# The merge of the two branches moved into the recurrent stage's block, its last head in column pieces, and semaphore counts that start at zero

## The chip, the cores and the metric

One core of one Trainium2 chip. The time is the device time of one launch in microseconds, all outputs written; lower is better. All times of the trace are microseconds from the start of the profiled execution.

## What is computed

A one-layer encoder step for a prompt of 1024 tokens and a sample of 64, 1088 tokens (T) in all, width 1024:

```python
h = rms_norm(x, norm_mix) * (1 + sc1) + sh1
hq, hf, hi, hog, gq, gk, gv, gog, glr, ga, gb = jnp.split(h @ w_in, split_at, axis=-1)
o_hg, s_hg = chunked_gated_linear_attention(q_hg, k_hg, hi, log_f, state_hgrn)     # 4 heads
o_gla, s_gla = chunked_gated_linear_attention(q_gla, gk, gv, log_g, state_gla)     # 4 heads
o = o * rsqrt(mean(o * o) + eps) * onorm * silu(gate)                              # both branches, per head
merged = sigmoid(ga) * (o_hg @ w_br_a) + sigmoid(gb) * (o_gla @ w_br_b)
x = x + g1 * (merged @ w_out)
x = x + g2 * hierarchical_moe(rms_norm(x, norm_ffn) * (1 + sc2) + sh2)             # 32 experts, 2 per token
y = rms_norm(x, norm_final)
```

Every product with a weight matrix is done as three matmuls of rounded parts (high x high, high x low, low x high; `split_matmul`, L131 to L135). So each operand is first split: a copy into a reduced type gives the high half, a subtraction the low half.

## The kernel before

Each stage is a block: the five engines run their own list of instructions and meet at the block's end, where all semaphores of the stage are cleared (`Stage.clear`, L121). The stages in order: conditioning (`condition`, names c_), the recurrent stage (`mixers`, x_), the merge (`merge`, m_), output projection and router (`out_router`, o_), experts (e_), overflow (v_), and the last norm (`combine`, z_). In each block SP first adds START = 20 to every semaphore of the stage, one instruction each (`raise_to_start`, L126), and every wait is written as `after(n)` or `landed(n)`, which add START.

**The recurrent stage** keeps the conditioned input h on chip as two halves, `h_hi` and `h_lo`, [128, 8, T] each. It goes through six units u: two of the GLA branch with two heads each, four of the HGRN branch with one head each. For a unit PE projects columns of `w_in` (`project`), each name in three column pieces (364, 364, 360) of 24 matmuls; GpSimd (POOL) makes the high half of each weight block (L510), VectorE (DVE) the low half (`next_low`, L1031); ScalarE (ACT) copies each piece out of PSUM (L652). Then the unit runs over nine tiles of tokens, j = 0 to 8 for an HGRN unit. Per j: PE turns tile j + 1 (L536, L538) and computes its scores (L552, L555), does a projection piece where the table `filled` puts one, then the outputs and the state product of tile j (L576 to L578). DVE masks the scores of tile j + 1 (L999, L1004, L1006: two reductions) and advances the state by tile j (L1019), which the outputs of j + 1 wait for. ACT copies tiles and outputs out of PSUM. Of the last unit (u = 5) the second gate block, x1, is projected in these gaps, its three pieces at j = 0, 3 and 6.

After the last tile: ACT squares the head's output, PE forms the mean over the 128 channels in three pieces (L585), ACT takes logarithm (L768) and exponential (L772), DVE multiplies by it and by the gate (L989, L992), and the row goes to scratch memory, like the seven head rows before (`scratch_mix`) and the 16 gate rows (`scratch_gate`). ACT waits for all of these to land, and the block ends.

**The merge** loads the eight head rows [128, T] back over ACT's queue through three buffers, splits them (L1180 on ACT, L1195 on DVE), and loops over the eight column blocks of 128, two per round of a hardware loop. Per column block and piece PE computes branch a (12 matmuls), then branch b (12), into two banks each, DVE multiplies each by its gate and adds (L1203, L1205, L1207); after the third piece ACT makes the high half (L1187) and DVE the low half (L1209) of the merged row. Weights of the block are halved by POOL alone (L1169, L1172). The first product of a column block waits for the last gate of the block before:

```python
pe.wait_ge(w_lo_done, after(2 * i + j + 1))
for c, (c0, n) in enumerate(COLS):

    pe.wait_ge(b_gated, after(n0 + max(c - 1, 0)))
```

## Time and profile before

| | |
|---|---|
| median of 3 runs | 1918.81 us (1918.67 to 1918.93) |
| the profiled execution | 1918.63 us, of which the span is 1916.8 |
| PE busy | 1617.3 us (84%), 10704 matmuls |
| DVE busy | 1274.5 us (66%) |
| ACT busy | 953.3 us (50%) |
| POOL busy | 323.6 us (17%) |
| granted TensorE clock, mean | 0.924 of 2.4 GHz |
| read from memory, written | 316.71 MB, 44.38 MB |

A line of a timeline is: start, duration, engine, line of the kernel, operation, what it writes <- what it reads, partitions x elements, count, and in brackets how long the engine had been idle and what ended that. SPq and ACTq are issues of transfers on these engines' queues. A line of the split into windows gives the busy time of each engine with its number of instructions, then the granted clock (1.00 is 2.4 GHz, 0.50 is 1.2 GHz), the busy share of the DMA engines and GB/s.

### The profile page before, as it was taken

Reading aid. Unit: us, or ns where it says so; the run is one execution under the profiler, and the core shown is the slowest. Engines: PE = TensorE matmul, PEld = TensorE weight load, DVE = VectorE, ACT = ScalarE, POOL = GpSimd, SP = SyncE. Lnnn points to the kernel's source line nnn. Section 1 sums busy time; section 2 is a strip of 40 time slices with the busy share of each in tenths; the row PEclk is TensorE's granted clock in tenths of the full one; section 3 lists DMA queues with packets and bytes.
Section 4 is the critical chain, followed back from the end, with each engine's and each line's share of the span. In section 5 each row is a group of like instructions: output and inputs, shape, how many; then the busy total and the mean of one; then the engine's idle time right before and its main releaser. Section 6 shows DMA issues by size and latency. Waiting matters only on the chain. (4 is left out here: it accounts for less than half of the span.)

```text
span 1916.8 us, 26572 instructions
## 1 busy us (share of the span) xinstructions
PE 1617.3 (84%) x10704; PEld 1413.7 (74%) x10704; DVE 1274.5 (66%) x1507; ACT 953.3 (50%) x1159; POOL 323.6 (17%) x186
## 2 busy tenths in 40 slices
PE   4579999999899998985696996499999999999800
PEld 2459989988789898984696785388888888887600
DVE  2534368267658575855454436789999999998727
ACT  2724234332625353443102211478888888888623
POOL 0100001000101010100220000134442332322113
PEclk8789999999999999998698998699999999999955
DMA  8722101201111202111542534699999999999546
GB/s 337 292 57 68 35 12 64 88 25 35 60 47 36 70 23 73 34 51 52 182 137 90 201 121 136 234 344 370 377 376 382 378 360 372 367 371 373 200 177 234
DMA packets 189073, 347.06 MB, mean 181 GB/s; under 512 B 18290, under 2 KB 74202, under 8 KB 187868
## 3 DMA queue, kind: packets, MB, share of 16 engines
q1 hardware_dynamic: 171676, 308.48, 45.4%
q10 hardware_dynamic: 7392, 19.06, 2.6%
q0 software_dynamic: 9888, 17.88, 2.5%
q8 instruction: 83, 1.36, 0.3%
q14 instruction: 34, 0.28, 0.0%
HBM read 316.71 MB, written 44.38 MB: 188 GB/s over the span
## 5 line engine op out<-in xcount | busy, mean ns | idle before, releaser
L133 PE MATMUL x_psum_proj<-h_hi,x_w_hi 128*128 128x364 f32 (+1 forms) x1056 | 362.7, 343 | 23.6 <-ACT x_v L652 11.8
L134 PE MATMUL x_psum_proj<-h_lo,x_w_hi 128*128 128x364 f32 (+1 forms) x1056 | 351.3, 333 | 0.0
L135 PE MATMUL x_psum_proj<-h_hi,x_w_lo 128*128 128x364 f32 (+1 forms) x1056 | 351.0, 332 | 0.0
L133 PEld LDWEIGHTS x_psum_proj<-h_hi,x_w_hi 128*128 128x128 f32 x1056 | 202.1, 191 | 32.5 <-ACT x_v L652 12.7
L134 PEld LDWEIGHTS x_psum_proj<-h_lo,x_w_hi 128*128 128x128 f32 x1056 | 202.4, 192 | 2.3
L135 PEld LDWEIGHTS x_psum_proj<-h_hi,x_w_lo 128*128 128x128 f32 x1056 | 202.1, 191 | 0.0
L510 POOL CAST x_w_hi<-x_w 128x1024 fp32r<-128x1024 f32 x44 | 73.1, 1661 | 664.6 <-PE x_psum_proj L135 662.2
L1751 POOL DMA_INDIRECT scratch_y<-e_y,all_tbl x32 | 79.6, 2486 | 392.3 <-ACT e_y L1825 367.8
L1006 DVE TENSOR_REDUCE x_sc<-x_diag 64x64 f32<-64x448 f32 x136 | 126.9, 933 | 1.1
L133 PE MATMUL e_psum_g<-e_g_hi,e_x_hi 128*128 128x512 f32 x256 | 105.9, 414 | 19.3 <-DVE e_x_lo L1901 18.9
L999 DVE TENSOR_TENSOR x_diag<-x_psum_sc,all_shapes 128x448 f32<-128x448 f32 (+1 forms) x72 | 44.6, 620 | 97.8 <-PE x_psum_sc L555 93.9
L1031 DVE TENSOR_TENSOR x_w_lo<-x_w,x_w_hi 128x1024 fp32r<-128x1024 f32 x44 | 53.6, 1221 | 83.6 <-POOL x_w_hi L510 83.5
L133 PE MATMUL e_psum_y<-e_d_hi,e_hid_hi 128*128 128x512 f32 x256 | 103.3, 404 | 5.4 <-DVE e_d_lo L1896 5.4
L134 PE MATMUL e_psum_g<-e_g_lo,e_x_hi 128*128 128x512 f32 x256 | 102.3, 400 | 0.0
L135 PE MATMUL e_psum_g<-e_g_hi,e_x_lo 128*128 128x512 f32 x256 | 101.8, 398 | 0.0
L134 PE MATMUL e_psum_y<-e_d_lo,e_hid_hi 128*128 128x512 f32 x256 | 100.6, 393 | 0.0
L135 PE MATMUL e_psum_y<-e_d_hi,e_hid_lo 128*128 128x512 f32 x256 | 100.6, 393 | 0.0
L135 PE MATMUL e_psum_u<-e_u_hi,e_x_lo 128*128 128x512 f32 x256 | 99.8, 390 | 0.0
L133 PE MATMUL e_psum_u<-e_u_hi,e_x_hi 128*128 128x512 f32 x256 | 99.6, 389 | 0.0
L134 PE MATMUL e_psum_u<-e_u_lo,e_x_hi 128*128 128x512 f32 x256 | 99.6, 389 | 0.0
L1745 POOL DMA_INDIRECT e_xg<-scratch_h,all_src x32 | 65.6, 2051 | 197.1 <-DVE e_xg L1854 165.4
L652 ACT ACTIVATE x_x<-x_psum_proj 128x364 f32<-128x364 f32 (+1 forms) x48 | 22.1, 469 | 136.4 <-PE x_psum_proj L135 136.3
(322 smaller groups left out, 3887.2 us busy)
## 6 DMA issues: line engine op xcount, KB each, us to landing
mg_ring_hi<-in_w_e_gate SPq DMA_DIRECT2D x34, 1024.0 KB, 14.3
mg_ring_lo<-in_w_e_down SPq DMA_DIRECT2D x34, 1024.0 KB, 15.1
mg_ring_hi<-in_w_e_up SPq DMA_DIRECT2D x32, 1024.0 KB, 11.9
mg_ring_lo<-in_w_e_up SPq DMA_DIRECT2D x32, 1024.0 KB, 13.6
mg_ring_lo<-in_w_e_gate SPq DMA_DIRECT2D x30, 1024.0 KB, 14.3
mg_ring_hi<-in_w_e_down SPq DMA_DIRECT2D x30, 1024.0 KB, 14.3
c_w<-in_w_ada SPq DMA_DIRECT2D x12, 2048.0 KB, 15.3
x_w<-in_w_in SPq DMA_DIRECT2D x44, 512.0 KB, 3.9
```

Of the source, the lines that this page charges most:

```text
L133: nc.tensor.matmul(out, lhs[0], rhs[0], start=start, stop=False)
L134: nc.tensor.matmul(out, lhs[0], rhs[1], start=False, stop=False)
L135: return nc.tensor.matmul(out, lhs[1], rhs[0], start=False, stop=stop)
L510: nc.gpsimd.tensor_copy(w_hi[:, n % 2], w[:, n % 2]).then_inc(w_hi_done, 1)
L652: nc.scalar.activation(dst[:, c0:c0 + n], p_proj[:, e % 2, 0:n], ACT.Copy).then_inc(proj_kept, 1)
L999: V.tensor_tensor(diag[0:n, j % 2], p_sc[0:n, j % 2, 0:NL * 64].rearrange("p (l t) -> p l t", t=64), masks[0:n], ALU.mult).then_inc(sc_mas ...
L1006: red = V.tensor_reduce(sc[h0:h0 + 64, j % 2, h0:h0 + 64], diag[h0:h0 + 64, j % 2].rearrange("p l t -> p t l"), AX.X, ALU.add)
L1031: V.tensor_tensor(w_lo[:, n % 2], w[:, n % 2], w_hi[:, n % 2].bitcast(F32), ALU.subtract).then_inc(w_lo_done, 1)
L1745: nc.gpsimd.indirect_dma_start(out=xg[:, e % 2, :], out_offset=None, in_=h2_d, in_offset=bass.IndirectOffsetOnAxis(ap=src[:, e:e + 1], axi ...
L1751: nc.gpsimd.indirect_dma_start(out=y_d, out_offset=bass.IndirectOffsetOnAxis(ap=tbl[:, e:e + 1], axis=0), in_=y[:, e % 2, :], in_offset=No ...
```

## The change

The merge becomes the tail of the recurrent stage's block; the stage between is gone, and its hardware loop is written out. In its parts:

- **Places.** The merged halves `mg_hi`, `mg_lo` get a fixed place at the top of the memory, over buffers that the last unit no longer needs (k, q, b, ke, qe, v1, g1, the levels); the sum `mg_sum` lies where `mg_lo` will be written. The head rows come back into the place of `h_lo` (`land`), once the last projection is done, and their halves take the place of `h_hi` and `h_lo`. Weights go through the stage's own two buffers: high half on POOL, low half on DVE. Gate rows go into buffers of the unit.
- **Seven rows instead of eight.** Rows 4 to 7 (branch b) and 0 to 2 come from scratch; row 3, the head of the last unit, stays on chip and is normed, gated and split in three column pieces.
- **Order on PE.** x1 of the last unit is projected at j = 0, 1, 2. Branch b of column block 0 starts before the outputs of the last tile; the mean squares stand between its pieces; then branch a without row 3, then with it. Blocks 1 to 7: three pieces of b, then three of a, in three banks each.
- **DVE.** Four of the low halves of head rows stand in the last unit at j = 4 to 7, three behind it; the low weight half of block 0 stands at j = 1, that of block i + 1 behind the first a gate of block i.
- **ACT.** The logarithms of the last gate row move to j = 6 to 8; the last merged row is split by pieces.
- **Counts from zero.** `raise_to_start` is called only in the overflow stage (whose loops wait on registers); everywhere else waits are for n itself, and `reach` leaves out a wait for 0.

The core of the diff (waits that only lose START are shown once; the functions `last_square`, `mix_low`, `last_output`, `last_low`, `gate_b`, `gate_a`, `merged_low` hold one or two instructions with their waits, as described above):

```diff
+def reach(eng, sem, n):
+        eng.wait_ge(sem, n)
 ...
-            raise_to_start(sp, s)
 ...
-                    sp.wait_ge(w_lo_done, after(n - 1))
+                    reach(sp, w_lo_done, n - 1)
 ...
 
 
+        if u + 1 == NU:
+            return [g for some in groups[j:j + 1] for g in some]
 ...
+        land = h.over("land", "lo", 0, [P, KD, T])
+        gates = [(v[1], g[1])] + [(t1, tg) if i % 2 else (x[0], x[1]) for i in range(1, KD)]
 ...
+        NB, LAST, MIX_ROWS = KD // 2, HG_HEADS - 1, [4, 5, 6, 7, 0, 1, 2]
+        bank_a, bank_b = [p_sc[:, 0], p_sc[:, 1], p_o[:, 1]], [p_proj[:, 0], p_proj[:, 1], p_o[:, 0]]
 ...
+            def branch_weights(i):
+                n = len(loads) + i
+                sp.wait_ge(w_lo_done, n - 1)
+                for half in range(2):
+                    sp.dma_start(w[:, n % 2, half * NB:(half + 1) * NB], w_branch[half][:, :, i * P:(i + 1) * P]).then_inc(w_in[n % 2], 16)
+            def gate_rows(i):
+                for half in range(2):
+                    sp.dma_start(gates[i][half][:, :], gate_d[i + half * KD]).then_inc(gate_in[i % 2], 16)
+            branch_weights(0)
+            branch_weights(1)
+            sp.wait_ge(gate_out[0], 16 * (G0[NU] // 2))
+            sp.wait_ge(gate_out[1], 16 * (G0[NU] // 2 - 1))
+            sp.wait_ge(o_out[1], out_landed(NU, 1))
+            gate_rows(0)
+            sp.wait_ge(proj_done, len(order))
+            sp.wait_ge(o_out[0], out_landed(NU - 1, 0))
+            for n, row in enumerate(MIX_ROWS):
+                sp.dma_start(land[:, row, :], mix_d[row]).then_inc(land_in[n // NB], 16)
+            branch_weights(2)
+            sp.wait_ge(last_scaled, NC)
+            sp.wait_ge(x_dve, G0[NU])
+            gate_rows(1)
+            sp.wait_ge(gate_out[1], 16 * (G0[NU] // 2))
+            gate_rows(2)
+            for i in range(3, KD):
+                branch_weights(i)
+                sp.wait_ge(piece_done, (i - 1) * NC)
+                gate_rows(i)
 ...
+            def branch_high(i):
+                n = len(loads) + i
+                pool.wait_ge(w_in[n % 2], 16 * (len(loads) // 2 + 2 * (i // 2 + 1)))
+                if i < 2:
+                    pool.wait_ge(proj_done, place[loads[n - 2], NC - 1] + 1)
+                else:
+                    pool.wait_ge(a_done, (i - 1) * NC)
+                nc.gpsimd.tensor_copy(w_hi[:, n % 2], w[:, n % 2]).then_inc(w_hi_done, 1)
+            branch_high(0)
+            branch_high(1)
+            for n, row in enumerate(MIX_ROWS):
+                pool.wait_ge(land_in[n // NB], 16 * NB if n < NB else 16 * (len(MIX_ROWS) - NB))
+                nc.gpsimd.tensor_copy(h_hi[:, row, :], land[:, row, :]).then_inc(mix_hi_done, 1)
+            for i in range(2, KD):
+                branch_high(i)
 ...
+            def branch_b(i, c):
+                pe.wait_ge(w_lo_done, len(loads) + i + 1)
+                if i:
+                    pe.wait_ge(b_gated, (i - 1) * NC + c + 1)
+                elif c < 2:
+                    pe.wait_ge(proj_kept, len(order))
+                else:
+                    pe.wait_ge(o_kept, J0[NU])
+                for row in range(NB, KD):
+                    if i == 0 and c == 0:
+                        pe.wait_ge(mix_lo_done, row - NB + 1)
+                    m = branch_product(i, row, c, bank_b[c], row == NB, row == KD - 1)
+                m.then_inc(b_done_m, 1)
+            def branch_a(i, c, rows):
+                if i:
+                    pe.wait_ge(a_gated, (i - 1) * NC + c + 1)
+                elif c < 2:
+                    pe.wait_ge(sc_masked, J0[NU])
+                    pe.wait_ge(cross_ready, X0[NU])
+                for row in rows:
+                    if i == 0 and c == 0 and row != LAST:
+                        pe.wait_ge(mix_lo_done, NB + row + 1)
+                    if i == 0 and row == LAST:
+                        pe.wait_ge(last_lo, c + 1)
+                    m = branch_product(i, row, c, bank_a[c], row == 0, row == LAST)
+                if row == LAST:
 ...
                     for (of, name), c in filled(u, j):
                         project(of, name, c)
+                    if u + 1 == NU and j + 1 == NS[u]:
+                        branch_b(0, 0)
                     outputs(u, j)
+            branch_b(0, 1)
+            last_square(0)
+            last_square(1)
+            branch_b(0, 2)
+            last_square(2)
-            for c in range(NC):
-                mean_square(NU - 1, 0, c)
+            for c in range(NC):
+                branch_a(0, c, range(LAST))
+            for c in range(NC):
+                branch_a(0, c, [LAST])
+            for i in range(1, KD):
+                for c in range(NC):
+                    branch_b(i, c)
+                for c in range(NC):
+                    branch_a(i, c, range(NB))
 ...
+                nc.scalar.activation(t1[:, c0:c0 + n], t1[:, c0:c0 + n], ACT.Exp, scale=-0.5).then_inc(last_exp, 1)
+            for c, (c0, n) in enumerate(COLS):
+                act.wait_ge(last_ready, c + 1)
 ...
+                    if u + 1 == NU and NB <= j < 2 * NB:
+                        mix_low(j - NB)
                 if u + 1 < NU:
                     decay_sum(u + 1)
+            for n in range(NB, len(MIX_ROWS)):
+                mix_low(n)
+            last_output(0)
+            last_output(1)
+            last_low(0)
+            last_output(2)
+            last_low(1)
+            last_low(2)
+            gate_x(NU - 1, NX[NU - 1] - 1)
+            for i in range(KD):
+                dve.wait_ge(gate_in[i % 2], 32 * (i // 2 + 1))
+                for c in range(NC):
+                    gate_b(i, c)
+                if i:
+                    merged_low(i - 1, 0, T)
+                for c in range(NC):
+                    gate_a(i, c)
+                    if c == 0:
+                        next_low()
+                    if i + 1 == KD and c:
+                        merged_low(i, *COLS[c - 1])
+            merged_low(KD - 1, *COLS[NC - 1])
-            gate_x(NU - 1, NX[NU - 1] - 1)
-            output(NU - 1, 0)
 ...
-def merge(nc, a, mix_d, gate_d, m_hi, m_lo):
 ...
-            m_hi, m_lo = m.sb("hi", [P, KD, T], F32R), m.sb("lo", [P, KD, T], F32R)
-            merge(nc, a, scratch["mix"], scratch["gate"], m_hi, m_lo)
```

How the engines' lists change. VectorE at the end of the last unit, before (L1019 is the state update, L974 the gate row, L989 and L992 the head's output; then the merge's block with the head rows' low halves):

```order
L1019 SCALAR_TENSOR_TENSOR x_state<-x_state,x_eb_last,x_psum_u 128x128 x2
L974 SCALAR_TENSOR_TENSOR x_x<-x_x,x_tg 128x1088
L989 TENSOR_TENSOR x_v<-x_v,x_t 128x1088
L992 SCALAR_TENSOR_TENSOR x_v<-x_v,all_onorm,x_g 128x1088
L91 UNCONDITIONAL_BRANCH
L1190 UNCONDITIONAL_BRANCH
L1195 TENSOR_TENSOR m_mix_lo<-m_mix,m_mix_hi 128x1088 x8
L1196 UNCONDITIONAL_BRANCH
L1196 ISA
```

and after the change, at the same place behind the head rows' low halves (L1190 and L1193 are an output piece, L1199 its low half, L1117 the gate row, L1206 a gate of branch b, L1212 of branch a, L1174 the low half of weights):

```order
L1193 SCALAR_TENSOR_TENSOR x_v<-x_v,all_onorm,x_g 128x364
L1199 TENSOR_TENSOR h_lo<-x_v,h_hi 128x364
L1190 TENSOR_TENSOR x_v<-x_v,x_t 128x360
L1193 SCALAR_TENSOR_TENSOR x_v<-x_v,all_onorm,x_g 128x360
L1199 TENSOR_TENSOR h_lo<-x_v,h_hi 128x364
L1199 TENSOR_TENSOR h_lo<-x_v,h_hi 128x360
L1117 SCALAR_TENSOR_TENSOR x_x<-x_x,x_tg 128x1088
L1206 TENSOR_TENSOR mg_sum<-x_g,x_psum_proj 128x364 x2
L1206 TENSOR_TENSOR mg_sum<-x_g,x_psum_o 128x360
L1212 TENSOR_TENSOR x_v<-x_v,x_psum_sc 128x364
L1214 TENSOR_TENSOR mg_sum<-mg_sum,x_v 128x364
L1174 TENSOR_TENSOR x_w_lo<-x_w,x_w_hi 128x1024
```

The head rows' low halves and the head's output now stand in one list without a block's end between them, and the weights of block 1 come behind all of them. SP's queue, before (the block's end and the loop's head lie between the weights of the projections, L496, and those of the merge):

```order
L496 DMA x_w<-in_w_in 128x8x128 x44
L91 UNCONDITIONAL_BRANCH
L1145 UNCONDITIONAL_BRANCH
L1148 UNCONDITIONAL_BRANCH
L1148 ISA
L1154 ISA
L1154 DMA m_w<-in_w_br_a 128x4x128
L1155 DMA m_w<-in_w_br_b 128x4x128
```

and after (L524 are branch weights, L528 gate rows, L539 head rows):

```order
L517 DMA x_w<-in_w_in 128x8x128 x44
L524 DMA x_w<-in_w_br_a 128x4x128
L524 DMA x_w<-in_w_br_b 128x4x128
L524 DMA x_w<-in_w_br_a 128x4x128
L524 DMA x_w<-in_w_br_b 128x4x128
L528 DMA x_v<-scratch_gate 128x1088
L528 DMA x_g<-scratch_gate 128x1088
L539 DMA h_land<-scratch_mix 128x1088 x7
L524 DMA x_w<-in_w_br_a 128x4x128
L524 DMA x_w<-in_w_br_b 128x4x128
L528 DMA x_t<-scratch_gate 128x1088
L528 DMA x_tg<-scratch_gate 128x1088
```

The gate rows of block 0 and two blocks of weights now stand ahead of the head rows, the gate rows of blocks 1 and 2 behind them.

## Rows read from the trace of the kernel before

**Rows 1.** Split into windows around the seam and in the merge, columns as told above.

```profile
910.00:920.00 10.00, 0.15 (x1) 0.18 (x2) 3.88 (x3) 3.31 (x4) 3.88 (x2) 0.50 1.01 353
...
920.00:930.00 10.00, 5.51 (x17) 4.88 (x18) 4.44 (x4) 3.97 (x4) 3.96 (x2) 0.50 1.04 358
...
960.00:980.00 20.00, 19.38 (x117) 19.08 (x116) 11.61 (x16) 1.66 (x2) 5.07 (x3) 1.00 0.47 161
```

**Rows 2.** Timeline of DVE in the last unit.

```profile
874.07 0.61 DVE L999 TENSOR_TENSOR x_diag<-x_psum_sc,all_shapes 128x448 f32<-128x448 f32 x1
...
877.02 0.61 DVE L999 TENSOR_TENSOR x_diag<-x_psum_sc,all_shapes 128x448 f32<-128x448 f32 x1
...
879.99 1.28 DVE L984 TENSOR_TENSOR x_g<-x_g,x_tg 128x1088 f32<-128x1088 f32 x1
...
888.57 0.35 DVE L1019 SCALAR_TENSOR_TENSOR x_state<-x_state,x_eb_last,x_psum_u 128x128 f32<-128x128 f32 x1 [1.29 <-PE x_psum_u L578]
```

**Rows 3.** Timeline of PE in the last unit.

```profile
860.88 0.27 PE L536 MATMUL x_psum_tok<-all_ident,x_ke 128*128 128x128 f32 x1
...
862.26 0.49 PE L576 MATMUL x_psum_o<-x_qe,x_state 128*128 128x128 f32 x2
...
863.03 0.27 PE L536 MATMUL x_psum_tok<-all_ident,x_ke 128*128 128x128 f32 x1
...
865.53 0.46 PE L576 MATMUL x_psum_o<-x_qe,x_state 128*128 128x128 f32 x2 [1.03 <-DVE x_state L1019]
```

**Rows 4.** Timeline of DVE and ACT at the merge's end.

```profile
1034.84 0.53 DVE L1205 TENSOR_TENSOR m_part<-m_gate,m_psum_b 128x360 f32<-128x360 f32 x1 [1.47 <-PE m_psum_b L135]
...
1036.06 1.11 ACT L1187 ACTIVATE mg_hi<-m_merged 128x1088 f32 x1 [11.74 <-DVE m_merged L1207]
...
1037.32 1.29 DVE L1209 TENSOR_TENSOR mg_lo<-m_merged,mg_hi 128x1088 f32 x1 [1.39 <-ACT mg_hi L1187]
```

**Rows 5.** Timeline of PE between two column blocks of the merge.

```profile
958.33 0.43 PE L133 MATMUL m_psum_a<-m_mix_hi,m_w_hi 128*128 128x364 f32 x1 [0.62 <-DVE m_part L1205]
```

**Rows 6.** The split into windows where the granted clock falls and returns.

```profile
836.00:840.00 4.00, 4.00 (x18) 4.00 (x18) 3.93 (x4) 3.22 (x6) 0.00 (x0) 0.63 0.00 0
...
840.00:844.00 4.00, 4.00 (x25) 4.00 (x24) 1.63 (x3) 0.47 (x1) 1.04 (x1) 0.94 0.34 139
...
888.00:892.00 4.00, 1.41 (x6) 0.59 (x4) 0.35 (x1) 3.75 (x5) 0.00 (x0) 0.96 0.00 0
```

**Rows 7.** Groups of instructions on the tile x_t: duration ns min/median/max, first and last start.

```profile
L585 PE MATMUL x_psum_tok<-x_t,x_mean x48: 465/468/947, 313.6 to 896.4; 128*128 128x364 f32 x32, 128*128 128x360 f32 x16
...
L768 ACT ACTIVATE x_t<-x_psum_tok,all_eps x24: 543/551/568, 315.2 to 897.3; 128x364 f32<-128x364 f32 x16, 128x360 f32<-128x360 f32 x8
```

**Rows 8.** Timelines of POOL and DVE: a cast beside an add.

```profile
957.87 1.04 POOL L1169 CAST m_w_hi<-m_w 128x1024 fp32r<-128x1024 f32 x1 [9.16 <-PE m_psum_b L135]
...
958.30 0.99 DVE L1207 TENSOR_TENSOR m_merged<-m_merged,m_part 128x360 f32<-128x360 f32 x1
```

**Rows 9.** Timelines at the start of four stages: another engine, then SP's first transfer.

```profile
4.44 0.20 POOL L212 MEMSET all_ident<- 128x128 f32 x1 [3.61 <-POOLq L2278]
...
6.32 0.31 SPq L191 DMA_DIRECT2D c_c_rows<-in_c_prompt  x1
...
97.34 0.20 POOL L500 MEMSET x_ones<- 128x128 f32 x1 [1.62 <-POOLq L123]
...
100.98 0.39 SPq L489 DMA_DIRECT2D x_lr_w<-in_w_in  x1
...
1039.43 0.13 POOL L1347 MEMSET o_m_before<- 128x32 bf16 x1 [26.46 <-POOLq L123]
...
1042.16 0.34 SPq L1302 DMA_DIRECT2D o_h<-in_shapes  x1
...
1843.71 1.28 ACT L2188 ACT_TABLE_LOAD   x1 [5.63 <-PEq L123]
...
1844.88 0.82 SPq L2154 DMA_DIRECT2D z_g<-scratch_mod  x2
```

More of the change, by code:

```diff
@@ L358, in _ @@
                 ada(j)
-            pe.wait_ge(ada_kept, after(FIRST))
+            reach(pe, ada_kept, FIRST)
             for j in range(FIRST):
@@ new lines, in branch_product @@
+            def branch_product(i, row, c, out, start, stop):
+                c0, n = COLS[c]
+                slot = (len(loads) + i) % 2
+                return split_matmul(nc, out[:, 0:n], (w_hi[:, slot, row, :], w_lo[:, slot, row, :]),
+                                    (h_hi[:, row, c0:c0 + n], h_lo[:, row, c0:c0 + n]), start, stop)
+            def branch_b(i, c):
[11 more added lines that the diff above has]
+                m.then_inc(b_done_m, 1)
@@ L2295, in program @@
                     for kind, o in (("hg", (outs[2], outs[4])), ("gla", (outs[3], outs[5])))}
[L2296 removed]
+            mixers(nc, a, h, h_hi, h_lo, m_hi, m_lo, merged, ident, scratch["mix"], scratch["gate"], rows, consts)
         with Stage(nc, "mg") as m:
[L2298 to L2299 removed]
+            m.starts.update(hi=MERGED_AT, lo=MERGED_AT + 4 * KD * T)
+            m.sb("fence", [P, 2 * KD * T], side="right")
             early = {"stage": m, "w_in": [m.sem(f"w_in{i}") for i in range(RING)],
```

678 lines of the change are left out of this document (321 added, 357 removed).

## The prediction

> **What bounds the kernel now.** I read the split into windows first. Around the end of the recurrent stage TensorE (PE) falls silent: in 910 to 920 us it is busy 0.15 of 10 us, in 920 to 930 it works at half clock, and only in 960 to 980 is it dense, 117 matmuls in 19.38 us, 0.166 us each [rows 1]. The timelines then date the seam. The last state update of the last unit starts at 888.57 [rows 2], the merge's last product reaches VectorE (DVE) at 1034.84 and the last low half starts at 1037.32 and takes 1.29 [rows 4], so the merge ends at 1038.6. Between 888.9 and 1038.6 lie 149.7 us for 8 x 72 = 576 matmuls, which at 0.166 are 95.7. So some 54 us of this seam are not matmul work: the head's norm, the way out to memory, the block's end, eight rows and the first weights loaded again, a cold clock, and 0.62 us before each group, where PE waits for the gate of the group before [rows 5]. Inside the unit the bound is DVE: one mask with its update takes 877.02 - 874.07 = 2.95 us [rows 2], while PE needs 1.38 for turn and scores and 0.77 for the outputs [rows 3].
>
> **1. The last unit, dated anew.** PE up to 860.88, where it turns tile 2, is as before. The three x1 projections now stand at j = 0, 1, 2 (before 0, 3, 6). From 860.88: scores 1.38, 24 matmuls 4.0, outputs 0.8, scores 1.4, projection 4.0, outputs 0.8, scores 1.4: 874.6, when DVE can mask j = 4 [rows 3]. From there DVE has four masks with updates (11.8), the half mask of the last tile (half the rows of the reduction: I estimate 1.5) with update (0.3), two gate operations of 1.2 (the pitch at 879.99) and, new, four low halves of the mix rows. These have the shape and kind of the gate operation, two SBUF inputs of 128x1088, so 1.2 each, 4.8 [rows 2]. Sum 21.0: 895.6. The weight half that DVE takes over at j = 1 stands where DVE waits for PE and costs nothing there. The scratch rows are asked for when the last projection is done, at 872.4: four rows are 2.23 MB, 6.3 us at the 353 GB/s of [rows 1]; I allow 2 us more for the way, for which I show no row, so they are there at about 881, when the first low half is due (881.7). That is just in time.
>
> **2. The clock.** In 888 to 892 PE was busy 1.41 of 4 us and the clock began to fall, and in 836 to 840, at a unit's boundary, it stood at 0.63 [rows 6]. From j = 3 on PE now does 2.15 us of work per 4 to 5.4 us of DVE. I take it as fallen to 1.2 GHz before the first branch products. There a matmul takes 5.51/17 = 0.32 us [rows 1]: the last quarter of the first branch-b piece and the final outputs cost about 2 us after 895.6, and the last update ends at 897.9, against 888.9 before. So **the unit gets 9.0 us longer**.
>
> **3. The tail of branch 0.** PE: second b piece, cold at first, 3.5, to 901.3; two mean squares of 0.47, third b piece 2.0, third mean square: 904.6 [rows 7]. ACT: logarithm 0.55 and exponential 0.5 per piece [rows 7], done at 905.6. DVE meanwhile: three more low halves 3.6 (901.5), then from 902.7 two pieces of output, 2.1, to 904.8. ACT's first high half is ready at 906.1; two low pieces, one output piece, a low piece with a short wait: 908.7. Then gate x 1.2, three b gates 1.6, first a gate and add 1.07 [rows 4], and only then the low half of the weights of branch 1, 1.2: 913.7. PE has finished branch 0 at 904.6 + 36 x 0.166 = 910.6 and waits 3.1 us for those weights. After it the clock is low again: what 836 to 844 shows as missing, (0.37 + 0.06) x 4 = 1.7 us [rows 6], is my price.
>
> **4. Branches 1 to 7.** 7 x 72 x 0.166 = 83.7 us on PE. DVE needs for one branch 3 x 0.53, 3 x 1.07, 1.2 and 1.3 to 2.0: 7.3 to 8.0 of 12.0. The b banks are free six matmul groups ahead, so the 0.62 of [rows 5] goes. Weights of branch i + 1 are cast when branch i - 1 is done, 12 us ahead; gate rows (1.1 MB, 3.2 us at 353 GB/s) have 12 us. All hidden. If that cover fails, each late weight is paid in full by PE. End of PE: 913.7 + 1.7 + 83.7 = 999.1.
>
> **5. The close.** Only one piece is left after the last product: gate and add 1.07, ACT 0.5, low half 0.53, hand-overs 0.2: 1001.4. Before it was a whole row, 1.11 on ACT and 1.29 on DVE [rows 4]. Against 1038.6 this is **-37.2 us**.
>
> **6. POOL against DVE.** The merge's cast ran from 957.87 to 958.91, and the add of two SBUF inputs that DVE began at 958.30 took 0.99 us instead of the 0.53 of its kind: it ended about when the cast let it [rows 8]. Seven casts of mix rows now run on POOL between 881 and 890, beside the gate scale and the low halves. Bounds: nothing (the casts fit into masks, which read PSUM), or four collisions of a full cast, 4.4. I take **+1.1**, nearest to the row's half cast, twice. The Trainium skill, SBUF — State Buffer, section SBUF: two separate sides, says that such a DVE operation and a GpSimd operation that reads SBUF exclude each other for the whole instruction; here the trace agrees, with 0.46 us. By that rule with every collision at its worst the change would be 3.3 us dearer.
>
> **7. Counts from zero.** In every block SP first raised each semaphore; other engines show when the block began. SP's first DMA came 6.32 - 4.44 = 1.9 us late in the conditioning, 100.98 - 97.34 = 3.6 in the recurrent stage, 1042.16 - 1039.43 = 2.7 in the output stage, 1844.88 - 1843.71 = 1.2 in the last [rows 9]. Each stage opens with a wait for these loads, so **-9.4 us**. In the expert stage SP's first load waits for a free slot anyway: 0, at most a gain of 0.9. The overflow stage keeps its raises. The two other pieces, the removed block end and the reload, are already inside the dates above. State rows and the last gate row go out under PE's work: nothing.
>
> **Sum.** -37.2 + 1.1 - 9.4 = -45.5. The profiled execution is 1918.63 us (span 1916.8 and 1.8 around it), the median 1918.81, 0.2 above. 1918.6 - 45.5 = **1873.1 us**, said as 1873.
>
> **Rivals.**
> *The clock holds.* For it: the pause of 1.03 us at 865.53 [rows 3] passed at full clock. Against: [rows 6]. It gives back the 1.7, and 2.4 of the tail (cold b pieces that delay the norm): 1873.1 - 4.1 = 1869.0.
> *Rows late, engines in each other's way.* The seven rows share the queue with weights; if the first four land 4 us late, DVE stands with the unit behind it, and all collisions add 3.3: 1880.4.
> *The raises were not on the path.* The conditioning, output and last stages are fed by long loads; if only the recurrent stage, whose PE starts after its first small loads, gets faster, 5.8 us are missing: 1878.9. Against: these loads run back to back from the first issue on, so a late start moves the end.
> *The change does not do what it says,* that is, PE still waits for all of branch 0's norm before any product. The order shows b pieces before the last outputs, so this can cost only the 6 us of b work: 1879.
> *The other side, slower: the clock stays low through the merge.* If a 3 us pause like the one before branch 1 returns before every branch, PE never gets back to 2.4 GHz and 504 matmuls cost 0.32 instead of 0.166: +80, less the 1.7 counted: 1951. It needs a late weight half in each branch; it decides once cast and low half together are later than 12 us. A branch's two gate rows take 3.2 us by [rows 1] and its two weight loads 1.5, so I hold it for unlikely.
>
> **How the numbers follow.** Forecast as it stands 0.50; clock holds 0.17; rows late or collisions 0.14; raises not paid 0.10; order of work not as told 0.03; slower 0.02; and 0.04 for something in the stages behind that shifts by more than 0.2%. A measurement here can tell about 0.2%, 3.8 us. The range reaches down to the clock rival and 3 us more (the bounds of the lock and of the expert stage), 1865, and up past the late rows, 1882. Faster 0.96, same 0.01, slower 0.03.
>
> **What would show it.** After the change: no idle stretch of more than 3.5 us on PE between 850 and 1000; the b pieces start near 885 to 890 (shifted by 5.5 for the raises) and the last update near 892; one PE wait of about 3 us released by DVE's weight half, and none later; 12 us per branch; 128x1088 low halves of 1.3, sometimes 2 us, between the masks; last low half near 997; SP's first DMA in each stage within 0.1 us of the other engines. I am wrong if a wait for the scratch rows stands on DVE in the last unit, if PE waits before each branch, or if the stages behind the merge don't shift by the same amount.

## The result and the profile after

The changed kernel takes **1875.93 us** (median of 4 runs, 1872.94 to 1876.96) against 1918.87 for the kernel before (4 runs, 1918.67 to 1919.62): a ratio of 0.9773, 95% interval 0.9756 to 0.979, so 42.9 us less. Forecast was 1873.0 with a range of 1865 to 1882. The profiled execution took 1875.47 us, with a span of 1873.7. PE was busy 1612.4 us, DVE 1280.9, ACT 945.4, POOL 318.7; the mean clock rose from 0.924 to 0.934 of 2.4 GHz.

**Around the seam**, the split into windows answers to [rows 1, 6] (busy time and number of instructions of PE, PEld, DVE, ACT, POOL, then granted clock, DMA share, GB/s):

```profile
884.00:888.00 4.00, 2.65 (x15) 2.26 (x16) 3.97 (x4) 1.44 (x4) 4.00 (x4) 0.68 0.00 1
...
892.00:896.00 4.00, 3.64 (x16) 3.16 (x15) 3.59 (x5) 1.27 (x2) 0.00 (x0) 0.57 0.00 0
...
908.00:912.00 4.00, 1.23 (x8) 0.93 (x6) 3.97 (x7) 1.11 (x1) 1.04 (x1) 1.00 0.54 121
912.00:916.00 4.00, 3.73 (x13) 3.73 (x14) 2.17 (x5) 1.11 (x1) 0.00 (x0) 0.59 0.96 333
...
960.00:980.00 20.00, 20.00 (x123) 20.00 (x122) 11.35 (x19) 2.23 (x2) 2.08 (x2) 1.00 0.40 138
```

The silence of [rows 1] is gone. In the kernel before it was one wait of PE, for the first weights of the merge:

```profile
919.85 0.64 PE L133 MATMUL m_psum_a<-m_mix_hi,m_w_hi 128*128 128x364 f32 x1 [22.61 <-POOL m_w_lo L1172]
```

After the change no wait of PE in the seam is longer than 4.10. What is left of it are two low stretches, one while DVE walks through the last tiles (0.68 and 0.57) and one behind a pause near 910 (0.59); from 920 on PE is full, 20.00 of 20 us.

**The last unit and the tail of branch 0** on DVE, as in [rows 2]:

```profile
880.17 2.15 DVE L1181 TENSOR_TENSOR h_lo<-h_land,h_hi 128x1088 fp32r<-128x1088 f32 x1 [1.22 <-POOL h_hi L579]
...
885.17 1.31 DVE L1127 TENSOR_TENSOR x_g<-x_g,x_tg 128x1088 f32<-128x1088 f32 x1
886.40 2.17 DVE L1181 TENSOR_TENSOR h_lo<-h_land,h_hi 128x1088 fp32r<-128x1088 f32 x1
...
891.39 1.28 DVE L1181 TENSOR_TENSOR h_lo<-h_land,h_hi 128x1088 fp32r<-128x1088 f32 x1
...
897.28 0.35 DVE L1162 SCALAR_TENSOR_TENSOR x_state<-x_state,x_eb_last,x_psum_u 128x128 f32<-128x128 f32 x1 [1.66 <-PE x_psum_u L649]
...
904.82 0.54 DVE L1199 TENSOR_TENSOR h_lo<-x_v,h_hi 128x364 fp32r<-128x364 f32 x1 [1.35 <-ACT h_hi L1032]
...
911.00 1.22 DVE L1174 TENSOR_TENSOR x_w_lo<-x_w,x_w_hi 128x1024 fp32r<-128x1024 f32 x1
```

The first low half waits 1.22 us for POOL's cast of the row, two low halves take 2.15 and 2.17 instead of 1.28, and the weight half of branch 1 comes at 911.00, behind everything else. Between 878.6 and 915 DVE pauses only where a bracket says so: it sets the pace here.

PE at the two pauses, and where the output stage begins:

```profile
885.35 0.72 PE L647 MATMUL x_psum_o<-x_qe,x_state 128*128 128x128 f32 x2 [4.10 <-DVE x_state L1162]
...
912.27 0.43 PE L140 MATMUL x_psum_proj<-h_hi,x_w_hi 128*128 128x364 f32 x1 [3.04 <-DVE x_w_lo L1174]
...
1008.56 0.80 PE L140 MATMUL o_psum_m<-o_w_hi,mg_hi 128*128 128x512 f32 x1 [10.86 <-DVE o_w_lo L1623]
```

No line between 912.27 and the merge's last product at 997.70 has a bracket: the 0.62 us of [rows 5] is gone from every block. POOL's casts, for which DVE waited, and the transfers for which POOL waited (SP's issue, then POOL):

```profile
869.82 3.27 SPq L539 DMA_DIRECT2D h_land<-scratch_mix  x7
```

```profile
879.04 10.49 POOL L579 CAST h_hi<-h_land 128x1088 fp32r<-128x1088 f32 x7 [8.07 <-DMA h_land<-scratch_mix]
```

The merge's end on DVE, which answers to [rows 4]; it is over at 999.93 (before 1038.61), with the last two pieces in one line:

```profile
998.75 1.18 DVE L1219 TENSOR_TENSOR mg_lo<-mg_sum,mg_hi 128x364 fp32r<-128x364 f32 x2
```

The starts of the four stages of [rows 9], POOL or ACT first and SP's first transfer behind it: 4.47 and 4.47, then the two below, then 1801.46 and 1801.44.

```profile
95.83 0.20 POOL L553 MEMSET x_ones<- 128x128 f32 x1 [1.62 <-POOLq L130]
...
1001.09 0.12 POOL L1444 MEMSET o_m_before<- 128x32 bf16 x1 [26.10 <-POOLq L130]
```

```profile
95.82 0.36 SPq L510 DMA_DIRECT2D x_lr_w<-in_w_in  x1
...
1001.09 0.33 SPq L1399 DMA_DIRECT2D o_h<-in_shapes  x1
```

**Where the 43.1 us of span went.** For a mark just ahead of the last unit I take POOL's 44th and last cast of projection weights, the same instruction in both kernels:

```profile
841.62 1.04 POOL L510 CAST x_w_hi<-x_w 128x1024 fp32r<-128x1024 f32 x1 [17.59 <-PE x_psum_proj L135]
```

```profile
838.74 1.04 POOL L563 CAST x_w_hi<-x_w 128x1024 fp32r<-128x1024 f32 x1 [17.60 <-PE x_psum_proj L142]
```

From the start of that cast to the end of the merge's last low half is called **the seam** from here on.

| stretch | before | after | difference |
|---|---|---|---|
| start to POOL's start of the recurrent stage | 97.34 | 95.83 | -1.51 |
| from there to SP's first transfer | 3.64 | -0.01 | -3.65 |
| from there to the 44th cast | 740.64 | 742.92 | +2.28 |
| the seam | 196.99 | 161.19 | **-35.80** |
| to the output stage's start | 0.82 | 1.16 | +0.34 |
| output stage (to ACT's start of the expert stage) | 168.41 | 166.83 | -1.58 |
| expert stage | 628.95 | 625.52 | -3.43 |
| overflow stage | 6.92 | 8.02 | +1.10 |
| last stage | 73.09 | 72.24 | -0.85 |
| span | 1916.8 | 1873.7 | -43.1 |

### The profile page after: what moved, and what is told of

The parts are those of the page before. It is cut to its first block and busy times, and to the rows that moved or that the text cites. A ratio compares the mean times of both kernels' runs of the same rounds, so it can differ in the third digit from the quotient of the medians.

```text
span 1873.7 us, 26133 instructions
## 1 busy us (share of the span) xinstructions
PE 1612.4 (86%) x10704; PEld 1412.8 (75%) x10704; DVE 1280.9 (68%) x1523; ACT 945.4 (50%) x1158; POOL 318.7 (17%) x185
## 5 line engine op out<-in xcount | busy, mean ns | idle before, releaser
L140 PE MATMUL x_psum_proj<-h_hi,x_w_hi 128*128 128x364 f32 (+1 forms) x1120 | 386.1, 345 | 27.0 <-ACT x_v L785 11.8
L141 PE MATMUL x_psum_proj<-h_lo,x_w_hi 128*128 128x364 f32 (+1 forms) x1120 | 374.2, 334 | 0.0
L142 PE MATMUL x_psum_proj<-h_hi,x_w_lo 128*128 128x364 f32 (+1 forms) x1120 | 373.9, 334 | 0.0
L140 PEld LDWEIGHTS x_psum_proj<-h_hi,x_w_hi 128*128 128x128 f32 x1120 | 215.8, 193 | 37.3 <-ACT x_v L785 12.7
L141 PEld LDWEIGHTS x_psum_proj<-h_lo,x_w_hi 128*128 128x128 f32 x1120 | 215.8, 193 | 2.5 <-issue 0.3
L142 PEld LDWEIGHTS x_psum_proj<-h_hi,x_w_lo 128*128 128x128 f32 x1120 | 215.5, 192 | 0.0
L1847 POOL DMA_INDIRECT scratch_y<-e_y,all_tbl x32 | 86.2, 2692 | 383.7 <-ACT e_y L1921 383.7
L1174 DVE TENSOR_TENSOR x_w_lo<-x_w,x_w_hi 128x1024 fp32r<-128x1024 f32 x52 | 63.4, 1221 | 81.0 <-POOL x_w_hi L563 80.9
```

Of the source, the lines that this page charges most:

```text
L140: nc.tensor.matmul(out, lhs[0], rhs[0], start=start, stop=False)
L141: nc.tensor.matmul(out, lhs[0], rhs[1], start=False, stop=False)
L142: return nc.tensor.matmul(out, lhs[1], rhs[0], start=False, stop=stop)
L1174: V.tensor_tensor(w_lo[:, n % 2], w[:, n % 2], w_hi[:, n % 2].bitcast(F32), ALU.subtract).then_inc(w_lo_done, 1)
L1847: nc.gpsimd.indirect_dma_start(out=y_d, out_offset=bass.IndirectOffsetOnAxis(ap=tbl[:, e:e + 1], axis=0), in_=y[:, e % 2, :], in_offset=No ...
```

## The experiments

Total times of kernels with this change scatter by up to 3 us around their median (1872.94 to 1876.96 above), so the small differences are read from the seam, in one trace each. The first question is whether the seam can bear that.

**The changed kernel again** (no edit).

> The changed kernel itself, for a second trace. From the tenth before-last weight cast of the recurrent stage (POOL's 44th cast of weights, 838.74 in the first trace) to the end of the merge's last low half it took 161.2 us. My theory says that this stretch depends on the order of the work alone and repeats within 0.5 us, while what lies ahead of it moves by 1 to 2 us with the place where the low clock falls, and the expert stage by 1 to 5 us with late weights. Rival: the stretch itself scatters by 1 to 2 us as the whole run does.

Measured: 1875.77 us (4 runs, 1874.8 to 1876.76), ratio 0.9785 [0.977, 0.9799]. The seam was 161.13 against 161.19, though the stretch from SP's first transfer to the 44th cast took 743.88 against 742.92. The expert stage, expected to move by 1 to 5 us, took 625.12 against 625.52. In this one repeat the seam agrees within 0.1 us, and the rival is out. A part of it does scatter between kernels that are alike up to there: DVE's wait for the first head row was 1.22 and 1.19 us in these two, 1.40 with the weight half earlier and 1.79 with the last head as one row. So 0.6 us of a difference between two seams can be chance.

**Counts from zero alone**, on the kernel before:

```diff
-            raise_to_start(sp, s)
...
-            act.wait_ge(small_in, landed(3))
+            reach(act, small_in, landed0(3))
```

> The kernel before with one part of the change alone: semaphores count from zero in the conditioning, recurrent, output, expert and last stages; the merge stage stays as it was. The forecast's term 7 says 9.4 us less (1909.4). What the changed kernel's trace suggests instead: the loads start earlier by 1.9 (conditioning), 3.6 (recurrent), 2.7 (output) and 1.2 (last), but the end of each stage moves less, 1.5, then 5.2 at the first products of the recurrent stage but only 2.9 in its last unit, because the low clock falls at another place in the program and lasts longer there: then 1.5 + 1.4 + 1.6 + 0.9 = 5.4 us less (1913.5). Rival: the clock's extra 2.3 us was caused by something else in the changed kernel, and the starts are worth their full 7.7: 1911.

The merge's and the overflow stage keep their raises. Measured: ratio 0.9959 [0.9945, 0.9972], 1908.07 us (5 runs) against 1916.3 on that chip: by the ratio 7.9 us less, between 5.4 and 10.5. The seam was 196.94, unchanged, as it must be. SP's first transfers stood beside the other engines (96.73 and 96.72 in the recurrent stage), and the stretch behind them took 740.90, not 742.92. So the 2.28 us that were lost after the start in the changed kernel's trace were no price of the starts: the rival is nearer, and counting from zero is worth about 8 us in all. The interval holds the 9.4 of term 7 too. Where the 8 us arise is not shown: against the one trace of before, the conditioning was 0.61 us shorter, the recurrent stage's start 3.65, the output stage 0.5 and the last 0.4, but the expert stage 5.5, for which term 7 had at most 0.9.

**The weight half of branch 1 earlier.** DVE does it ahead of the last head's first low piece.

```diff
             last_output(1)
+            next_low()
             last_low(0)
...
-                    if c == 0:
+                    if c == 0 and i:
                         next_low()
```

> The changed kernel with one DVE operation moved: the low half of the weights of branch 1 (1.2 us) stands ahead of the last head's first low piece, where DVE waits 1.35 us for ACT, and no longer behind the first a gate of branch 0. My theory: PE's wait of 3.04 us before branch 1 goes, with it the low clock behind it (1.7): 4.7 us less, 1871.2. Rival: the work ahead of it becomes the bound, so the last head's rows come 1.2 later and PE waits there instead: 3.0 to 3.5 less. Second rival: the clock dips anyway: 3.0 less.

Measured: ratio 0.9756 [0.9742, 0.9769], seam 156.91, 4.3 us less. DVE's gap of 1.35 took the operation, and the first low piece waited 0.22 instead:

```profile
900.94 1.22 DVE L1174 TENSOR_TENSOR x_w_lo<-x_w,x_w_hi 128x1024 fp32r<-128x1024 f32 x1
902.38 0.54 DVE L1199 TENSOR_TENSOR h_lo<-x_v,h_hi 128x364 fp32r<-128x364 f32 x1 [0.22 <-ACT h_hi L1032]
```

PE's timeline has no bracket behind branch 0 at all, and the clock stays up (1.00 in the windows 904:908 and 908:912):

```profile
908.00:912.00 4.00, 4.00 (x26) 4.00 (x26) 2.56 (x6) 1.11 (x1) 0.00 (x0) 1.00 0.96 316
```

Counted from the 44th cast, PE begins branch 1 2.7 us earlier (70.81 against 73.53), and its branches 1 to 7 take 83.87 instead of 85.43, 1.6 less. The prediction's 3.1 and 1.7 were the right two terms; the wait of 3.04 gave 2.7, as the last update came 0.2 later (a head row 0.18 later).

**Branch b last in block 0.**

```diff
-            branch_b(0, 1)
             last_square(0)
             last_square(1)
-            branch_b(0, 2)
             last_square(2)
...
             for c in range(NC):
                 branch_a(0, c, [LAST])
+            for c in range(NC):
+                branch_b(0, c)
```

(`branch_b(0, 0)` goes from the unit's last tile too, and POOL's cast for branch 2 also waits for the b products.)

> The changed kernel with the b branch of block 0 behind its a branch (blocks 1 to 7 as they were), so that no b product covers the last unit's end and the norm. My theory: PE has 36 matmuls, 6.0 us, less to do while the norm runs and does them behind it; the clock is low from the wait as well (1 to 2 us); 2 us come back because DVE's gates of branch 0 and the weight half of branch 1 already wait: 5 to 8 us more than the changed kernel, 1881 to 1884. Rival: DVE, not PE, sets the pace of this stretch (it has 1.4 us of waits in 20): then b first is worth nothing, and the time changes by less than 2 us.

Measured: 1879.86 us, ratio 0.9804 [0.9789, 0.9819], seam 166.43, 5.2 us more. DVE now stands behind PE for b, three times, and the weight half is as late as before:

```profile
910.96 0.53 DVE L1204 TENSOR_TENSOR mg_sum<-x_g,x_psum_proj 128x364 f32<-128x364 f32 x1 [3.00 <-PE x_psum_proj L142]
...
912.88 0.53 DVE L1204 TENSOR_TENSOR mg_sum<-x_g,x_psum_proj 128x364 f32<-128x364 f32 x1 [1.39 <-PE x_psum_proj L142]
...
914.88 0.53 DVE L1204 TENSOR_TENSOR mg_sum<-x_g,x_psum_o 128x360 f32<-128x360 f32 x1 [1.46 <-PE x_psum_o L142]
```

Branch b first is worth 5.2 us, somewhat less than its 36 products take (36 x 0.166 = 6.0). The rival, by which DVE alone set the pace, falls.

**The high halves on ACT.**

```diff
-            for n, row in enumerate(MIX_ROWS):
-                pool.wait_ge(land_in[n // NB], 16 * NB if n < NB else 16 * (len(MIX_ROWS) - NB))
-                nc.gpsimd.tensor_copy(h_hi[:, row, :], land[:, row, :]).then_inc(mix_hi_done, 1)
...
+                    if u + 1 == NU:
+                        for n in {5: (0,), 6: (1, 2, 3), 7: (4, 5), 8: (6,)}.get(j, ()):
+                            mix_high(n)
```

> The changed kernel with the seven high halves of the mix rows on ACT (1.1 us each) and not on POOL. My theory: the two low halves that took 2.15 and 2.17 us take 1.28, because POOL and DVE no longer share their port; the last update comes 1.7 us earlier (about 895.9 against 897.6), 1874.2. Rival: the low halves wait for the rows from scratch or for ACT, whose casts stand behind its own work, and nothing is gained: 1875 to 1877.

Measured: ratio 0.9775 [0.976, 0.979], not to be told from the changed kernel by the time; seam 160.16, 1.0 less. The low halves are short again, as my theory says:

```profile
878.93 1.29 DVE L1186 TENSOR_TENSOR h_lo<-h_land,h_hi 128x1088 fp32r<-128x1088 f32 x1 [1.14 <-ACT h_hi L912]
...
884.28 1.28 DVE L1186 TENSOR_TENSOR h_lo<-h_land,h_hi 128x1088 fp32r<-128x1088 f32 x1
...
895.07 0.35 DVE L1167 SCALAR_TENSOR_TENSOR x_state<-x_state,x_eb_last,x_psum_u 128x128 f32<-128x128 f32 x1 [2.40 <-PE x_psum_u L646]
```

But of the 1.7 us only 1.0 arrived: the last update waits 2.40 for PE instead of 1.66. A quarter of the first b piece stands ahead of the final outputs. DVE's fourth low half, which it needs, was there (it began at 891.39 and takes 1.28), but PE went through this quarter at the low clock, while in the changed kernel the clock was back by then. The last product of it, here and in the changed kernel:

```profile
893.50 0.51 PE L142 MATMUL x_psum_proj<-h_hi,x_w_lo 128*128 128x364 f32 x1
```

```profile
896.11 0.33 PE L142 MATMUL x_psum_proj<-h_hi,x_w_lo 128*128 128x364 f32 x1
```

**A semaphore for each row.**

```diff
-                sp.dma_start(land[:, row, :], mix_d[row]).then_inc(land_in[n // NB], 16)
+                sp.dma_start(land[:, row, :], mix_d[row]).then_inc(land_in[n], 16)
...
-                pool.wait_ge(land_in[n // NB], 16 * NB if n < NB else 16 * (len(MIX_ROWS) - NB))
+                pool.wait_ge(land_in[n], 16)
```

> The changed kernel with a semaphore for each of the seven mix rows from scratch instead of one for the first four and one for the last three, so that POOL can cast the first row when it alone is there. My theory: the first row lands some 3 to 4 us before the fourth, the cast starts at 875 to 876 instead of 879.04, DVE's wait of 1.22 us for it goes, and more of the casts fall beside masks: 1.2 to 2 us less in the stretch from the 44th weight cast to the merge's end (161.2 before, 159.2 to 160 now). Rival: the four rows move together on 16 engines and land within 1 us of each other: less than 0.5 us.

Measured: ratio 0.9766 [0.975, 0.9783], seam 159.80, 1.4 less. SP issued the rows from 870.04 on; POOL's first cast started 3.7 us later, the third at 877.96:

```profile
873.75 1.09 POOL L579 CAST h_hi<-h_land 128x1088 fp32r<-128x1088 f32 x1 [2.55 <-DMA h_land<-scratch_mix]
875.17 2.06 POOL L579 CAST h_hi<-h_land 128x1088 fp32r<-128x1088 f32 x1 [0.33 <-DMA h_land<-scratch_mix]
877.96 1.09 POOL L579 CAST h_hi<-h_land 128x1088 fp32r<-128x1088 f32 x1 [0.73 <-DMA h_land<-scratch_mix]
```

The rows land one after the other, and DVE's first low half has no wait. The rival falls. Here too PE did the last quarter of the first b piece at the low clock, and the last update waited 2.34 for it.

**The last head as one row.** DVE's two output operations, ACT's high half and DVE's low half work on 1088 columns at once, and PE waits for the one low half:

```diff
-                dve.wait_ge(last_exp, c + 1)
+                dve.wait_ge(last_exp, NC)
...
-                        pe.wait_ge(last_lo, c + 1)
+                        pe.wait_ge(last_lo, 1)
```

> The changed kernel with the last head scaled, split and taken over as one row of 1088 instead of in three column pieces. My theory: PE has a products of rows 0 to 2 until the pieces are there anyway (until 907.59, with the first low piece done at 905.4), so the pieces save little: the whole row's low half would be done about 0.4 us after that, and DVE has four operations fewer: the stretch from the 44th weight cast to the merge's end is 161.2 give or take 0.7. Rival, what the pieces are for: the first product with the last head comes 2.5 us later (about 908) and PE stands for the difference and drops its clock: 2 to 4 us more.

Measured: ratio 0.9771 [0.9756, 0.9786], which the time can't tell from the changed kernel; seam 163.83, 2.6 us more. Of these 0.6 is the first head row, later here ahead of anything that the edit touches, and 2.0 are the edit's (from the last update to branch 1, 17.03 us against 14.99). My theory was wrong, the rival right, at the lower end of its 2 to 4. PE, then DVE's wait for the row:

```profile
909.41 0.40 PE L140 MATMUL x_psum_sc<-h_hi,x_w_hi 128*128 128x364 f32 x1 [1.98 <-DVE h_lo L1195]
...
914.00 0.43 PE L140 MATMUL x_psum_proj<-h_hi,x_w_hi 128*128 128x364 f32 x1 [2.87 <-DVE x_w_lo L1173]
```

```profile
879.83 2.15 DVE L1180 TENSOR_TENSOR h_lo<-h_land,h_hi 128x1088 fp32r<-128x1088 f32 x1 [1.79 <-POOL h_hi L579]
```

I had put the whole row's low half 0.4 us behind the end of the other a products; PE stood 1.98. Four dependent steps over 1088 columns (1.29, 1.35, 1.11, 1.29) do not overlap, where the pieces of three engines do.

**Low halves on POOL**, on top of three edits already tried (high halves on ACT, a semaphore for each row, weight half early):

```diff
+            for n, row in enumerate(MIX_ROWS):
+                pool.wait_ge(mix_hi_done, n + 1)
+                nc.gpsimd.tensor_tensor(h_lo[:, row, :], land[:, row, :], h_hi[:, row, :].bitcast(F32), ALU.subtract).then_inc(mix_lo_done, 1)
...
-                    if u + 1 == NU and NB <= j < 2 * NB:
-                        mix_low(j - NB)
```

> Four edits together on the changed kernel: high halves of the mix rows on ACT, their low halves on POOL (taken from DVE), a semaphore for each row, and the weight half of branch 1 ahead of the last head's first low piece. My theory: DVE is the engine that sets the pace from the masks to the first gates; seven times 1.28 us, a wait of 1.2 and the shared port go from it. The last update comes 5 to 6 us earlier in the stretch, the merge's end 8 to 9 us earlier than in the changed kernel: 152 to 153 instead of 161.2, about 1867. Rival: POOL's subtraction takes over 2.5 us a row and blocks DVE's gate operations through the port, so branch b waits for POOL: 156 to 158, no better than the weight half alone (156.9).

Measured: **1865.89 us**, ratio 0.9732 [0.9719, 0.9746], seam 153.12, 8.1 less. My theory held for the seam (8 to 9 less), but the last update came only 3.5 us earlier (55.0 from the 44th cast, against 58.5), not 5 to 6, and the rival was right about the port. DVE's gate operation, then POOL:

```profile
878.16 3.45 DVE L1135 TENSOR_TENSOR x_g<-x_g,x_tg 128x1088 f32<-128x1088 f32 x1
```

```profile
874.96 2.50 POOL L579 TENSOR_TENSOR h_lo<-h_land,h_hi 128x1088 fp32r<-128x1088 f32 x1 [7.72 <-ACT h_hi L915]
877.96 15.89 POOL L579 TENSOR_TENSOR h_lo<-h_land,h_hi 128x1088 fp32r<-128x1088 f32 x6 [0.50 <-ACT h_hi L915]
```

POOL's second subtraction began at 877.96, 0.2 ahead of DVE's operation, which then took 3.45 instead of 1.28: it stood for 2.2 us, about the rest of POOL's.

**The same with DVE keeping the low halves** (`mix_low` as in the changed kernel).

> The changed kernel with three edits together: high halves of the mix rows on ACT, a semaphore for each row, the weight half of branch 1 ahead of the last head's first low piece; DVE keeps the low halves. Alone they took 1.0, 1.4 and 4.2 us from the stretch between the 44th weight cast and the merge's end (161.2). My theory: the unit and the tail are separate, so the weight half adds in full; the first two meet at the same DVE waits (1.14 us for a row was left with ACT's casts) and at PE's quarter of branch b, for which the last update waits longer the earlier DVE is: 154.5 to 155.5. Rival: they add up in full and the freed wait too: 153.4. Second rival: the last update stays bound by PE: 156.

Measured: **1866.59 us** (4 runs, 1861.36 to 1867.01), ratio 0.9732 [0.9712, 0.9751], seam 153.73, 7.5 less. The single gains sum to 4.3 + 1.0 + 1.4 = 6.7. This is the first rival's case, the full sum and more, not my part-sum. Of the excess of 0.8 the trace shows where it lies: DVE got back all that it had lost in the unit (1.22 + 0.87 + 0.89 = 2.98 us), the last update came 2.97 earlier, and it waited 1.67 for PE as in the changed kernel, where each of the two single edits made that wait 0.7 longer through PE's low clock. The first low half has no bracket, the last update a short one:

```profile
876.41 1.28 DVE L1186 TENSOR_TENSOR h_lo<-h_land,h_hi 128x1088 fp32r<-128x1088 f32 x1
...
891.83 0.35 DVE L1167 SCALAR_TENSOR_TENSOR x_state<-x_state,x_eb_last,x_psum_u 128x128 f32<-128x128 f32 x1 [1.67 <-PE x_psum_u L646]
```

**The gate scale ahead of POOL's subtractions.**

```diff
-                    if j == 5:
+                    if j == (4 if u + 1 == NU else 5):
                         gate_g_scale(u, SUB[u] - 1)
...
+            pool.wait_ge(g_dve, 2 * H0[NU])
```

> The kernel with lows on POOL, and the gate scale of the last unit one tile earlier, with POOL's first subtraction held back until it is done, because there the gate scale took 3.45 us instead of 1.28 while POOL subtracted. My theory: it takes 1.28 to 1.3 again, the fifth to last update and all after it come 2.1 us earlier, PE starts its unbroken work 2 us earlier: 151.0 to 151.5 in the stretch instead of 153.1. Rival: POOL's seven subtractions of 2.65 us, now 1.4 later, become the bound of branch b or of the first a products, PE waits 1 to 2 us for them, and the stretch stays at 152 to 153.

Measured: ratio 0.974 [0.9725, 0.9755], seam 152.82, only 0.3 less than with lows on POOL. The gate operation was 1.28 again and the last update came 1.9 us earlier (53.1 from the 44th cast, against 55.0), and yet the gain did not pass on. PE, then DVE:

```profile
889.13 0.43 PE L140 MATMUL x_psum_proj<-h_hi,x_w_hi 128*128 128x364 f32 x1 [1.58 <-POOL h_lo L580]
...
892.00 0.51 PE L142 MATMUL x_psum_proj<-h_hi,x_w_lo 128*128 128x364 f32 x1
```

```profile
877.80 1.28 DVE L1136 TENSOR_TENSOR x_g<-x_g,x_tg 128x1088 f32<-128x1088 f32 x1
...
896.23 0.62 DVE L1199 TENSOR_TENSOR x_v<-x_v,x_t 128x364 f32<-128x364 f32 x1 [5.14 <-ACT x_t L1038]
```

POOL, started later, is now what branch b waits for: the rival. Behind that wait the clock was low, and the second b piece took 3.5 us (890.63 to 894.12), where it took 2.1 with the gate scale in its old place; with it the mean squares, the exponential and DVE's output came later.

## Why the prediction was right

The time came out 2.9 us above the forecast and inside its range, and the likeliest case was the one that happened. The profiled execution was 2.4 above its 1873.1: 0.3 in the seam, 1.8 in the starts as this pair of traces has them, and 0.3 of what no step had. By its steps:

**1 and 2, the last unit.** From the mask of tile j = 4 to the last update the forecast had 23.0 us without step 6, 24.1 with it (874.6 to 897.55, plus 1.1); the trace has 25.5 (871.79 to 897.28). The lock cost 1.8 (2.15 + 2.17 - 2 x 1.28) instead of 1.1, and the rows were late by 1.22. The forecast let four rows take 8.6 us from issue (872.4 to 881); it was 9.2 (869.82 to 879.04), so the 2 us that it allowed for the way beside the 6.3 of its rate, without a row, were 2.9. With a semaphore for each row POOL's first cast stood 3.7 us behind the issue: what was late was not the first row but the fourth, for which the first was made to wait. So of the rival "rows late, engines in each other's way" a part came true, 1.22 + 0.7 us of its 7.3, and the sentence "I am wrong if a wait for the scratch rows stands on DVE in the last unit" named a wait that is there, if short. PE's longest pause was 4.10, not under 3.5. The clock did fall here, to 0.57, as step 2 took it, but it was back when the last quarter of the first b piece began (895.68). Step 1's terms for DVE add up to 20.8 us, not the 21.0 that it wrote.

**3, the tail.** PE was to wait 3.1 us for the weight half of branch 1 with a low clock behind it for 1.7: it waited 3.04, and moving that half away gave 4.3. Here the forecast was nearest to the trace. Its other low stretch was not there: the second b piece, taken as cold at 3.5 us, took 2.1 (897.18 to 899.27).

**4, branches 1 to 7.** 83.7 + 1.7 = 85.4 forecast, 997.70 - 912.27 = 85.4 measured. No wait in them, so neither the slower rival nor a late gate row had a place. An add beside POOL's weight cast does take longer (the 128x360 add of the merged row took 0.96 in five of the eight blocks, 0.53 in the others), and all of that lies under PE.

**5, the close.** 2.3 forecast, 2.2 measured (997.70 to 999.93). Steps 1 to 6 make -36.1; the seam says **-35.8**. That the sum is right to 0.3 is partly luck: the unit was 1.4 too long, the tail up to the end of branch 0 took 12.0 us from the last update instead of 13.0, and the too cold second b piece is what made up for the late row and the collisions. No run takes the 35.8 us apart further than b first (5.2) and the column pieces (about 2): that most of it is the block's end, the wait for memory and the reload is read from the two traces.

**7, counts from zero.** This is the term that is least certain in size. SP's starts came 1.9, 5.2 (1.5 passed on and 3.65 of its own), 2.7 and 1.2 us earlier, each within 0.1 us of the other engines as said (in the conditioning 32 increments of SP had stood 0.06 us apart, from 4.44 to 6.25). But of "a late start moves the end" only the recurrent stage's 3.65 is shown. In this pair of traces 1.51 of 1.9 passed in the conditioning, 1.58 of 2.7 in the output stage and 0.85 of 1.2 in the last, 7.6 of 9.4 in all; yet over the ten traces with the new merge the recurrent stage starts at 94.3 to 96.3, the output stage takes 165.3 to 168.5 and the last 71.4 to 73.3, and there is one trace of before. Alone on the kernel before the change was worth 7.9 us [5.4 to 10.5], which leaves room for the 9.4. It leaves none for the rival's 3.6, but half of that run's gain in its trace lay in the expert stage, so the total does not show that the long loads of the other three stages carried the rest.

**What no step had.** Outside the seam and the starts the two traces differ by +2.28 in the recurrent stage, -3.43 in the expert stage and +1.10 in the overflow stage. The first is within what traces of the same work differ by, shown below. For the second the forecast had 0 to 0.9. In the one trace of before ACT waits 7.5 us for expert weights from memory, against 1.1 after, and PE has waits of 0.54, 1.38 and 1.05 us near the stage's end where after has 0.15. Counts from zero alone left 623.48 of 628.95, and the ten traces with the new merge lie between 623.4 and 626.2, none with such waits of PE. So counting from zero may be worth more here than the forecast had, but one trace of before can't tell how much. The third is 6.9 and 6.8 us in the two kernels with the old merge and 8.0 to 8.6 in the ten traces with the new one; that stage's code is the same, and why it takes over 1 us longer stays open.

## What to carry to other kernels

When a stage is folded into the one ahead of it, list what the engine that sets the pace at the joint does in order: the largest single loss left here was one 1.2 us operation of DVE standing behind work that was not urgent, 4.3 us with the clock. Rows that are waited for in a group cost the time of the last one: a semaphore for each took 1.4 us off. Together three such edits, none of which removes work, bring the ratio to the kernel before from 0.9773 to 0.9732. Handing DVE's work to POOL gained only 0.6 us more in the seam: an engine that is freed helps only until the next one, here PE and then POOL, is the one waited for. And a saved microsecond in front of a PE at its low clock partly goes again: 0.7 us in two of the experiments, 1.4 in a third.

## What the runs showed of the hardware

**The same instructions take 740.6 to 744.1 us.** From SP's first transfer of the recurrent stage to the 44th cast no kernel here differs in its work, and the traces give, among others, 740.60, 741.73, 742.92, 743.88 and 744.08. It is the place at which the low clock meets the program. Near the stage's start PE pauses 0.55 us at a time (111.01 and 115.67 in the changed kernel, 116.69 and 121.36 before). The windows after that pause, before the change and then after it:

```profile
120.00:124.00 4.00, 3.34 (x13) 1.46 (x11) 0.00 (x0) 1.68 (x4) 0.00 (x0) 0.96 0.00 0
124.00:128.00 4.00, 4.00 (x16) 4.00 (x17) 0.00 (x1) 3.79 (x4) 0.00 (x0) 0.62 0.00 0
```

```profile
116.00:120.00 4.00, 3.89 (x10) 2.11 (x9) 0.00 (x0) 2.31 (x4) 0.00 (x0) 0.68 0.00 0
120.00:124.00 4.00, 4.00 (x15) 4.00 (x15) 1.14 (x1) 2.69 (x3) 0.00 (x0) 0.50 0.00 0
```

Before, the fall came late and most of the cheap products of 16 rows were through at full clock (six took 2.49 us); after, it took part of them (3.05) and then the first full ones up to 124.0, 5.4 us of them against 3.2: 1.1 us lost by the third weight cast (137.65 - 108.36 = 29.29 between second and third, against 133.55 - 103.13 = 30.42). A second such place is between the 25th and 26th cast, 22.78 us at a mean clock of 0.93 before and 23.85 at 0.86 after. The other 0.1 is spread. The Trainium skill, TensorE: Matmul & The Clock Gate, section What's actually happening, says that what watches the engine runs freely and isn't reset when a kernel starts. The spread of 3.5 us between equal stretches fits that; no run here tests it. So an edit that shifts a stage by a few microseconds also draws this lot anew, and a difference of 1 to 2 us in the total says nothing until the stretch that was edited is read by itself.

**POOL and DVE stand for each other.** An operation of DVE with two inputs on chip took 2.15 us beside a cast of 1.09 and 3.45 beside a subtraction of 2.5, in place of 1.28. POOL stood too: three of its seven casts took 2.15 us, where alone one takes 1.09. Masks and state updates, which read PSUM, kept their times (0.61 and 0.35 us). The loser stood for most of the other's instruction (0.87, 0.89 and 2.17 us), not half of it as step 6 had it. This agrees with the rule of the Trainium skill, SBUF — State Buffer, section SBUF: two separate sides, that the prediction named: one of the two is shut out for the whole instruction of the other.

**POOL's subtraction** of 128x1088 took 2.50 us against 1.28 on DVE, a factor of 1.95. GPSIMD Engine Reference of the Trainium skill, section 3.1, gives 1.96 for an addition of this kind; the trace agrees.
